# Reordering the head of a window attention: exponentials, past-key copy and first division each moved ahead of a rounding or subtraction

## What is computed

```python
s = jnp.einsum('bnqhgd,bnkhd->bnhgqk', qb, kb) * (SWA_HD ** -0.5)
m = jnp.maximum(jnp.max(s, axis=-1, keepdims=True), sk)     # sk: one learned sink logit per head
p = jnp.exp(s - m)
p = p / (jnp.sum(p, axis=-1, keepdims=True) + jnp.exp(sk - m))
o = jnp.einsum('bnhgqk,bnkhd->bnqhgd', p, vb)
```

```python
m = rmsnorm(mem, lw['mem_in_norm_g'])
k = rmsnorm((m @ lw['w_mk']).reshape(B, M, MEM_HEADS, MEM_HD), lw['mem_k_norm_g'])
v = (m @ lw['w_mv']).reshape(B, M, MEM_HEADS, MEM_HD)
```

## Time and profile before

| | us |
|---|---|
| median of three runs | 1838.91 |
| lowest, highest | 1833.05, 1839.54 |
| the profiled execution, its whole time | 1837.01 |
| its span in the profile | 1835.4 |
| the stage `window_and_memory` in it | about 531 to 634 |

### The profile page before, as it was taken

How to read it: one execution, slowest core, us unless ns; L and a number is a source line. 1 busy time by engine, 2 the same in 40 slices (tenths; PEclk the granted TensorE clock), 3 DMA queues, 4 the chain that set the end, 5 groups by cost and what they waited for, 6 DMA issues and landing times. The chain is left out here.

```text
span 1835.4 us, 27737 instructions
## 1 busy us (share of the span) xinstructions
PE 1767.6 (96%) x10347; PEld 1616.6 (88%) x10347; DVE 1166.7 (64%) x1378; ACT 780.7 (43%) x1490; POOL 736.9 (40%) x627
## 2 busy tenths in 40 slices
PE   6999999989989999999999989999999999999999
PEld 5999999988967788898788879999999999987787
DVE  6235655865765633423543278888888888799985
ACT  5016673325676432312143255444444444454432
POOL 4001212015544350211125028766666666457643
PEclk9999999999989999999999999999999999999999
DMA  5122111233245230124512222222222221596554
GB/s 174 49 59 63 36 36 49 87 95 106 66 137 171 102 144 24 47 104 149 185 58 81 69 66 72 71 74 72 72 73 73 71 73 64 206 348 195 160 178 142
DMA packets 166456, 188.05 MB, mean 102 GB/s; under 512 B 14065, under 2 KB 121178, under 8 KB 165944
## 3 DMA queue, kind: packets, MB, share of 16 engines
q1 hardware_dynamic: 165448, 186.55, 31.6%
q0 software_dynamic: 896, 0.19, 0.1%
q10 hardware_dynamic: 16, 0.00, 0.0%
HBM read 151.64 MB, written 35.07 MB: 102 GB/s over the span
## 5 line engine op out<-in xcount | busy, mean ns | idle before, releaser
L3771 PE MATMUL ffn_banks<-h_parts,up_hi 128*128 128x384 f32 x1920 | 489.6, 335 | 8.9 <-DVE h_parts L4269 5.2
L3771 PEld LDWEIGHTS ffn_banks<-h_parts,up_hi 128*128 128x128 f32 x1920 | 346.6, 188 | 11.3 <-issue 8.6
L3771 PE MATMUL ffn_banks<-h_parts,up_lo 128*128 128x384 f32 x960 | 321.5, 335 | 0.0
L4168 POOL TENSOR_TENSOR up_lo<-up_raw,up_hi 128x512 fp32r<-128x512 f32 x174 | 260.8, 1514 | 133.7 <-ACT up_hi L3933 89.3
L987 PE MATMUL proj_banks<-x_hi,in_w_hi 128*128 128x384 f32 x624 | 214.9, 344 | 0.5 <-DVE x_lo L251 0.5
L987 PE MATMUL proj_banks<-x_hi,in_w_lo 128*128 128x384 f32 x624 | 208.8, 335 | 0.0
L987 PE MATMUL proj_banks<-x_lo,in_w_hi 128*128 128x384 f32 x624 | 208.6, 334 | 0.0
L3771 PEld LDWEIGHTS ffn_banks<-h_parts,up_lo 128*128 128x128 f32 x960 | 180.6, 188 | 0.0
L4213 POOL TENSOR_TENSOR h_parts<-down_cells,h_parts 128x512 fp32r<-128x512 f32 x69 | 108.7, 1583 | 92.7 <-ACT h_parts L4006 92.7
L3892 PE MATMUL ffn_banks<-h_parts,up_hi 128*128 128x512 f32 x352 | 138.3, 393 | 3.6 <-DVE h L4441 2.3
L3895 PE MATMUL ffn_banks<-h_parts,up_lo 128*128 128x512 f32 x352 | 137.1, 390 | 0.0
(11 more groups left out here) (568 smaller groups left out, 3809.7 us busy)
## 6 DMA issues: line engine op xcount, KB each, us to landing
up_raw<-in_w_up SPq DMA_DIRECT2D x44, 512.0 KB, 3.9
down_cells<-in_w_down SPq DMA_DIRECT2D x58, 256.0 KB, 5.7
up_raw<-ffn_gated_rows SPq DMA_DIRECT2D x44, 320.0 KB, 5.5
ffn_gated_rows<-h SPq DMA_DIRECT2D x22, 576.0 KB, 2.8
in_w_raw<-in_w_in SPq DMA_DIRECT2D x24, 512.0 KB, 3.9
up_raw<-ffn_gated_rows SPq DMA_DIRECT2D x44, 256.0 KB, 3.3
spill<-mixT SPq DMA_DIRECT2D x10, 576.0 KB, 4.3
h_kept<-h SPq DMA_DIRECT2D x9, 512.0 KB, 2.6
```

The source lines that it names most:

```text
L3771: ins = nc.tensor.matmul(banks[:, bank, 0:TC], wt[:, j, k, :], parts[:, q, x, k, :], start=(fresh and n == 1), stop=(n == last), skip_grou ...
L4168: nc.gpsimd.tensor_tensor(w_lo[:, j], weights.full(j), w_hi[:, j].bitcast(F32), ALU.subtract).then_inc(weights.split[j], 1)
```

## The change

Three pieces are moved and none is added or removed.

1. ACT: the exponentials of the first tile stand ahead of the rounding of weight pair 0.
2. DVE: the copy of the turned past keys stands ahead of `low(4)` and `low(5)`, directly behind the first denominators.
3. POOL: the first division stands ahead of the subtraction of pair 0, and the subtraction of pair 2 and the second division stand ahead of the filling of the masked queries.

```diff
@@ DVE
             denominators(0)
-            for f in range(4, 6):
-                low(f)
             dve.wait_ge(past_turned, 1)
             nc.vector.tensor_copy(kpT, t_bank).then_inc(past_copied, 1)
-            for f in range(6, KD):
+            for f in range(4, KD):
                 low(f)
             weights_low(1)
             maxima(1)
@@ ACT
             for f in range(4):
                 high(f)
+            exponentials(0)
             weights_high(0)
-            exponentials(0)
             for f in range(4, KD):
                 high(f)
@@ POOL
+            normalize(0)
             weights_low(0)
-            normalize(0)
+            weights_low(2)
+            normalize(1)
             pool.wait_ge(m_turned, 4)
             nc.gpsimd.memset(masked_flat, 0.0).then_inc(cleared, 1)
             pool.wait_ge(cleared, 1)
             for j in range(2):
...
             ins.then_inc(masked_ready, 1)
-            weights_low(2)
-            normalize(1)
             weights_low(4)
```

## The result

The changed kernel took 1843.29 us (median of nine runs, 1840.14 to 1848.5). The kernel before took 1836.88 us in nine runs (1833.05 to 1839.54). The ratio is 1.0034 with a 95% interval of 1.0023 to 1.0046: **6.4 us slower**. The forecast was 1844.0 us and a loss of 6.2 us against the profiled execution's own time. The span went from 1835.4 to 1842.4 us. The interval leaves out 1, so a change of a third of a per cent is told from none here.

The account below looks back on a forecast made before the run. PE, busy 96% of the span, was taken as the bound, with POOL's subtractions setting the weight loads it waits for. Loss 4.6 + 1.6 = 6.2 us; from the middle of two bases, 1844.0 us, range 1837.5 to 1850.0.

Parts of the forecast that it names:

- Part 1: Tile 0's exponentials and first division: exponentials end 0.60 us earlier, division runs 541.57 to 543.46 instead of 542.38 to 544.27.
- Part 2: Past keys' copy on DVE: ends at 543.44, so turn(0) begins at 543.60, 0.98 us earlier, all the change can give.
- Part 3: POOL's pair 0 subtraction and the weight loads: pair 3's load leaves 2.97 us later; unit 6 loses 1.37 us.
- Part 4: POOL's lock with DVE: pair 1's subtraction ends at 546.9, pair 2's near 549.1, 0.2 us earlier, which nobody needs.
- Part 5: Second division ahead of masked queries' fill: pair 7's load leaves 4.3 us later, PE's unit 16 starts 4.6 us later.
- Part 6: PE's gap of about 5 us before unit 16 lowers its clock, costing 1.6 us (0 to 5.0).
- The sum: Whole kernel: 4.6 + 1.6 = 6.2 us slower, 1844.0 us; chance of the forecast as summed 0.55.
- Rival A: PE's clock stays up behind the gap: loss of 4.6 us without the 1.6, 1842.5 us; chance 0.13.
- rival C: Weight loads of pairs 3 and 7 are early enough after all: 0.7 us less, 1837.3 us; chance 0.07.
- D: Masked queries' block costs less and DVE and ACT catch up: loss of about 3 us, 1841.0 us; chance 0.12.
- B: PE's clock stays down for 10 us behind the gap: 4.6 + 5.0 = 9.6 us, 1847.5 us; chance 0.13.

Follow-up runs that it names:

- e10: Kernel before with only VectorE's edit, the past keys' copy ahead of low(4) and low(5); ratio 0.9992 (0.9980 to 1.0005) to the kernel before.
- e1: Changed kernel with GpSimd's order put back as before, leaving ACT's and VectorE's moves; ratio 1.0025 (1.0016 to 1.0034) to the kernel before.
- e8: Changed kernel with the fill of the masked queries moved behind pair 4's subtraction; ratio 1.0004 (0.9993 to 1.0016) to the kernel before.
- e2: Changed kernel with the fill back ahead of pair 2's subtraction, so only the first division stays moved on GpSimd; ratio 1.0011 to the kernel before.
- e3: Kernel before with only pair 2's subtraction and the second division ahead of the masked queries' fill; ratio 1.0031 (1.0019 to 1.0042) to the kernel before.
- e13: Kernel before with pair 2's subtraction and the second division ahead of the fill's four copies only, memset kept early; ratio 1.0013 to the kernel before.
- e4: Changed kernel with ACT's rounding of pair 7 behind the exponentials of tile 2 and rows_out(1); ratio 0.9998 (0.9990 to 1.0007) to the kernel before.
- e5: Kernel before with ACT's rounding of pair 7 behind the exponentials of tile 2 and rows_out(1); ratio 0.9988 (0.9976 to 1.0000) to the kernel before.
- e11: Kernel before with the past keys' copy ahead of low(4) and low(5) and pair 7's rounding behind rows_out(1); ratio 0.9998 to the kernel before.

## Why the prediction was right

By its own steps, with 0.60 taken off the start times after:

- **Part 1, right.** DVE's first addition took 0.16 us in place of 0.38 and the division ran 541.58 to 543.47, forecast 541.57 to 543.46.
- **Part 2, right, and its gain is small on its own.** `turn(0)` came 0.97 us earlier. e10 shows that the copy alone brings 0.2 of it and e1 that ACT's and VectorE's moves without GpSimd's turn it into a wait of 4.2 us.
- **Part 3, right.** Pair 3's load left at 545.83 (forecast 545.82), landed in 4.1 us, and unit 6 started at 552.30 (forecast 552.26). e8, where this stands nearly alone, puts it at 1.21 us for unit 16. e2's 1.66 us (2.0 in the timed runs) has a second cause, the late subtraction of pair 2.
- **Part 4, right in the change, missed in e3.** Pair 1's subtraction on DVE took 1.94 us and pair 2's on POOL 3.39 us (it ended at 549.14, forecast 549.1). What I did not see is that the lock's price depends on 0.05 us of order: e3 lost 1.8 us through it, e13 got them back. In the change pair 0's subtraction was already running when VectorE's came, so VectorE lost only 0.7 us and went ahead of pair 2's. I was wrong that nobody needs pair 2's earlier place: PE's unit 4 started 0.06 us behind the end of that subtraction after a wait of 0.24, and with pair 2 behind the fill, in e2, the wait was 1.82. It gave nothing in the end, as unit 6 had to wait for pair 3 all the same.
- **Part 5, right.** The memset began at 555.37 (forecast 555.4), fill and meeting took 2.97 us (forecast 3.04), pair 7's load left at 560.75 (forecast 560.92) and landed in 4.0. Unit 16 came 4.43 us late, forecast 4.6. e8, which moves the fill alone, takes 3.2 of it back, and e4 shows that only `exponentials(2)` and `rows_out(1)` standing behind pair 7 made it PE's business.
- **Part 6, right in kind, too small.** The four units behind the wait and `output(1)` took 575.56 - 568.99 = 6.57 us, against 568.02 - 563.96 = 4.06 before: 2.5 us, where I had put 1.6. I took the low stretch of 3.4 us from the earlier trace rows; it was 6.8 us in the change and 6.9 when run again, of which some fell into the wait itself. The twelve products of the four units start 0.44 us apart, in place of 0.24, from the first to the last, so the low clock lasted through all of them. It happened both times, and in e3 (windows of 0.76 and 0.56) behind a wait of 4.69 us.
- **The sum.** 4.43 + 2.51 = 6.94 us in the stage (101.92 - 95.02 = 6.90), against 6.2 forecast and 6.4 timed. Rival A (no clock) would have left 4.6, the faster rival C is excluded by the two load times, the half loss of D by unit 16's 4.43, and B's 10 us at the lower clock did not occur. That the total came within 0.7 us is in part luck: the base (the middle of 1837.01 and 1838.91) was 1.1 us above the median of the nine runs before, and the stage's loss was put 0.7 too low. That middle is 1837.96, which with 6.2 gives 1844.2 and not 1844.0. And the 0.5% that I took for the least that can be told from no change was too wide: the interval is 0.12% to either side.

That the stage's loss reaches the end in full rests on the spans (7.0 us more; 7.2 between the second profiles of the two kernels) and the ratios; the rest of the trace was not followed instruction by instruction.

## What to carry to other kernels

A subtraction on an engine with time to spare can be the one that frees a ring's buffer. Before moving anything ahead of it, follow the ring's load to the next instruction that needs it, and see what stands behind that one. Work that nobody waits for belongs in the gap it already has, or behind the subtraction that releases a load (one line moved took the loss from 0.34% to 0.04%). And a rounding that waits for a DMA should stand behind the work that doesn't, not ahead of it: that alone hid a load four microseconds late (e4).

## What the runs showed of the hardware that was not expected

- Which of two meeting subtractions stands still turned on a start 0.05 us earlier: 3.41 us on VectorE in e3 against 1.22 in e13, where VectorE's came first and POOL's was the longer (2.62).
- A memset on POOL, which left a two-input subtraction of VectorE alone in e13 (545.90, 1.22 long, beside the memset from 544.97 to 546.78), goes with a long record of a tiny one-input operation in the changed kernel: L2440 took 1.04 us in place of 0.16 and ended with the memset (557.80 and 557.78). It was so again in the second profile of the change and in e3 (1.05 us each). The subtraction behind it started before that end and took no longer than usual, so nothing was lost by it that the rows show. On DVE:

```profile
556.76 1.04 DVE L2440 TENSOR_SCALAR swa_nm<-swa_mx 128x4 f32<-128x4 f32 x1
557.12 1.23 DVE L2421 TENSOR_TENSOR mkv_w_lo<-mkv_raw,mkv_w_hi 128x1024 fp32r<-128x1024 f32 x1
```

  The Trainium skill ("SBUF — State Buffer", the section that explains its diagram of engine ports) says that a VectorE instruction in a two-port mode excludes any GpSimd instruction, while one with two SBUF inputs excludes only those that read SBUF; the memset beside the subtraction agrees with the second half, and L2440 with the first if it runs in such a mode, which no row shows.
- Behind each wait of PE of 4.19 us or more in this stage the clock fell to 1.2 GHz (e1, e3, the change twice). Behind waits of 1.8 to 2.4 us it fell in the profiles of e2, e8, e10 and e13. It stayed up behind such waits in those of e1, e3, e5 and e11 and in both of the kernel before. The single profile of e10 held two such falls and a stage 2.9 us longer, while its timed runs were no slower than before: a fall in one profile is not the kernel's time.
